# A hybrid conv, attention and mixture-of-experts step on one core: conditioning rows copied by ScalarE from two banks, tokens in three transfers, experts' weights placed in ten rounded columns

## What is computed

```
shift1, scale1, gate1, shift2, scale2, gate2 = split(silu(c) @ w_ada + b_ada)
h = rms_norm(x, norm1) * (1 + scale1) + shift1
conv_in, q_lat, kv_lat, k_rope, gates = split_projection(h @ w_in)
...                                  # conv branch, attention branch, merge
x = x + gate1 * ((g_conv * conv_out + g_att * att) @ w_out)
h2 = rms_norm(x, norm2) * (1 + scale2) + shift2
g_idx = argmax(h2 @ w_group); top two of the four experts of that group, weights comb
y = sum over the two experts of comb * (silu(h2 @ w1) * (h2 @ w3)) @ w2
x = x + gate2 * y
```

## Time and profile before

| | us |
|---|---|
| median of three runs | 976.42 |
| lowest, highest | 973.01, 978.05 |
| the profiled execution | 973.11 |
| its span in the trace | 971.3 |

### The profile page before, as it was taken

One profiled execution on the slowest core, in us unless ns is written; L12 is line 12 of the kernel. 1 busy time (PEld: TensorE's weight loads), 2 busy tenths in 40 slices (PEclk: granted clock), 3 DMA queues, 4 the chain that ended last, 5 costly groups with the idle time before them and its releaser, 6 DMA issues.

```text
span 971.3 us, 15302 instructions
## 1 busy us (share of the span) xinstructions
PE 920.6 (95%) x5910; PEld 776.3 (80%) x5910; DVE 737.4 (76%) x1208; ACT 512.0 (53%) x728; POOL 63.4 (7%) x62
## 2 busy tenths in 40 slices
PE   3999999989999899999989999998999989999997
PEld 1798889767898678888868988995589968788886
DVE  4665999564855799778967579995658568997895
ACT  4353822375522577647756346326663247774772
POOL 1000000064000000000010000001800000000000
PEclk9899999999999999999999999999999999999999
DMA  9943557401555689949927444531123247994961
GB/s 373 412 151 129 206 214 293 184 1 44 207 227 217 232 310 368 361 167 351 373 106 306 180 170 159 226 136 44 44 91 130 84 154 279 383 368 159 348 260 66
DMA packets 29018, 206.73 MB, mean 213 GB/s; under 512 B 3408, under 2 KB 3440, under 8 KB 4240
## 3 DMA queue, kind: packets, MB, share of 16 engines
q1 hardware_dynamic: 28656, 204.81, 55.2%
q0 software_dynamic: 288, 0.92, 0.3%
HBM read 203.98 MB, written 1.74 MB: 212 GB/s over the span
## 4 chain that ended last, share of the span: by engine, by line
PE 79%; DVE 10%; ACT 6%; issue 3%; DMA 1%; POOL 1%; ACTq 0%; SPq 0%; DVEq 0%
PE ps L875 59%; PE ps L886 4%; PE ps L862 3%; PE ps L1300 2%; PE ps L853 2%; DVE w_lo L743 2%; DVE w_lo L738 2%; ACT w_hi L732 2%; PE ps L1041 1%; PE ps L1129 1%; PE ps L1117 1%; POOL probs L832 1%; PE ps L1369 1%; PE ps L1370 1%; ACT kT L1563 1%
## 5 line engine op out<-in xcount | busy, mean ns | idle before, releaser
L743 DVE TENSOR_TENSOR w_lo<-ring,w_hi 128x2048 fp32r<-128x2048 f32 (+1 forms) x100 | 224.0, 2246 | 25.0 <-ACT w_hi L1670 24.5
L875 PE MATMUL ps<-h_hi,w_hi 128*128 128x384 f32 x576 | 198.0, 344 | 6.1 <-issue 2.4
L1670 ACT ACTIVATE w_hi<-ring 128x2048 fp32r<-128x2048 f32 x96 | 183.2, 1914 | 30.6 <-PE ps L875 30.6
L875 PE MATMUL ps<-h_hi,w_lo 128*128 128x384 f32 x576 | 193.6, 336 | 0.0
L875 PE MATMUL ps<-h_lo,w_hi 128*128 128x384 f32 x576 | 193.5, 336 | 0.0
L738 DVE TENSOR_TENSOR w_lo<-ring,w_hi 128x2048 fp32r<-128x2048 f32 x46 | 104.9, 2288 | 27.5 <-ACT w_hi L732 27.5
L875 PEld LDWEIGHTS ps<-h_hi,w_hi 128*128 128x128 f32 x576 | 108.0, 188 | 19.4 <-issue 11.7
L875 PEld LDWEIGHTS ps<-h_lo,w_hi 128*128 128x128 f32 x576 | 108.2, 188 | 0.0
L875 PEld LDWEIGHTS ps<-h_hi,w_lo 128*128 128x128 f32 x576 | 108.1, 188 | 0.0
L1916 DVE SCALAR_TENSOR_TENSOR z<-u,par,z 128x399 f32<-128x399 f32 x180 | 103.1, 629 | 0.9
L875 PE MATMUL ps<-w_hi,hg_hi 128*128 128x512 f32 x256 | 103.3, 404 | 0.0
(11 more groups left out here) (283 smaller groups left out, 1484.9 us busy)
## 6 DMA issues: line engine op xcount, KB each, us to landing
ring<-wpre SPq DMA_DIRECT2D x96, 1024.0 KB, 6.6
ring<-wmoe SPq DMA_DIRECT2D x96, 1024.0 KB, 5.8
x<-x SPq DMA_DIRECT2D x1, 1536.0 KB, 7.6
x_out<-x SPq DMA_DIRECT2D x4, 384.0 KB, 2.3
par<-par_in POOLq DMA_DIRECT2D x2, 367.5 KB, 6.8
const<-const_in SPq DMA_DIRECT2D x1, 314.0 KB, 3.2
ckv_out<-ckvT POOLq DMA_DIRECT2D x2, 64.0 KB, 3.7
kr_out<-kr POOLq DMA_DIRECT2D x2, 16.0 KB, 3.5
```

Source lines behind the costliest of these rows:

```text
L743: return nc.vector.tensor_tensor(out, whole, leading.bitcast(F32), ALU.subtract)
L875: m = mm(out, a, b, start=(start and i == 0 and j == 0), stop=(stop and i == n - 1 and j == 2))
L1670: af(w_hi[m % MOE_PLACES], slot(moe_slot(l, m)), ACT.Copy).then_inc(split_hi, 1)
```

## The change

- **Copies.** In layer 0 ScalarE takes over the copy of the conditioning rows from VectorE (`first_copy`), and the batches take turns in two banks (FIRST_BANKS), so that TensorE waits for the batch before the last only.
- **Order.** TensorE does the sum of squares first, then batches 0 and 1 whole, then the latent products of chunks 0 and 1; batches 2 and 3 follow with one chunk between rows and columns of each, and chunks 4 to 7 come last. ScalarE splits lat 1 behind chunk 1 (before: 3). VectorE makes the reciprocal in one instruction, without the copy between two parts.
- **Transfers.** Order is now cond, x in three parts (chunks 0 to 3, 4 and 5, 6 and 7), const. cond has its own semaphore, on which ScalarE's SiLU waits alone. GpSimd issues par only after the last part of x has landed.
- **Experts' weights.** VectorE splits `cwr` into two rounded halves (`cw_parts`, two more instructions and one more wait ahead of `cw_ready`); TensorE gathers the ten columns with fp32r operands; VectorE copies one half and adds the other (one more instruction).

```
-            sp.dma_start(cond_sb[:, :, :], cond).then_inc(loaded, 16)
+            sp.dma_start(cond_sb[:, :, :], cond).then_inc(cond_loaded, 16)
+            for (a, b), landed in zip(X_PARTS, x_loaded):
+                sp.dma_start(x[:, a:b, :], x0[:, a:b, :]).then_inc(landed, 16)
             sp.dma_start(const[:, :], const_in).then_inc(loaded, 16)
-
-            sp.dma_start(x[:, :, :], x0).then_inc(x_loaded, 16)
...
         def _(pool):
+            pool.wait_ge(x_loaded[-1], 16)
             pool.dma_start(par, par_in[0]).then_inc(par_loaded, 16)
...
-                    if k == 0:
-
-                        pe.wait_ge(adaT_taken, b)
-                    m = ada_rows_of(raw_unit("first", k * FIRST_STEPS + b), k, 2)
+                    if k == 0 and b >= len(FIRST_BANKS):
+
+                        pe.wait_ge(adaT_taken, b - len(FIRST_BANKS) + 1)
+                    m = ada_rows_of(raw_unit("first", k * FIRST_STEPS + b), k, 2, bank=FIRST_BANKS[b % 2])
...
                 if l == 0:
+                    square_sum()
                     first_rows(0, 0)
-                    square_sum()
                     first_rows(0, 1)
-                    ada_columns(1)
+                    ada_columns(1, bank=FIRST_BANKS[0])
+                    first_rows(1, 0)
+                    first_rows(1, 1)
+                    ada_columns(2, bank=FIRST_BANKS[1])
                     outs = [begin("lat", t) for t in range(TT)]
-                    for b in range(1, FIRST_STEPS):
+                    latent(0, outs)
+                    latent(1, outs)
+                    for b in range(2, FIRST_STEPS):
                         first_rows(b, 0)
                         first_rows(b, 1)
-                        ada_columns(b + 1)
-                        latent(2 * b - 2, outs)
-                        latent(2 * b - 1, outs)
-                    latent(KD - 2, outs)
-                    latent(KD - 1, outs)
+                        latent(b, outs)
+                        ada_columns(b + 1, bank=FIRST_BANKS[b % 2])
+                    for c in range(KD - 4, KD):
+                        latent(c, outs)
...
-                    n = EPG + 1
+                    n = 2 * (EPG + 1)
                     for b in range(PAIR):
-                        m = product(ps[:, 7, FE + b * n:FE + (b + 1) * n], [pick[:, t, b * P:(b + 1) * P].bitcast(F32) for t in range(TT)],
-                                    [cwr[:, t, :] for t in range(TT)])
+                        m = product(ps[:, 7, FE + b * n:FE + (b + 1) * n], [pick[:, t, b * P:(b + 1) * P] for t in range(TT)],
+                                    [cw_parts[:, t, :, :].rearrange("p s n -> p (s n)") for t in range(TT)])
...
+                def first_copy(b):
+                    act.wait_ge(ada_full, b + 1)
+                    if b:
+                        act.wait_ge(adaT_full, b)
+                    af(ada_rows, ps[:, FIRST_BANKS[b % 2], 0:ADA_COLS], ACT.Copy).then_inc(ada_taken, 1)
...
+                    if l == 0:
+                        first_copy(0)
+                        act.wait_ge(loaded, 16)
                     hi(1 if l > 0 else 0)
...
-                        if l == 0 and c == 3:
+                        if l == 0 and c == 1:
+                            first_copy(1)
                             hi(1)
+                        if l == 0 and c in (3, 5):
+                            first_copy(c // 2 + 1)
...
+                    mark(nc.vector.reciprocal(rs[:, 0:TOK], rs[:, 0:TOK]))
                     if l == 0:
-                        mark(nc.vector.reciprocal(rs[:, CTX:TOK], rs[:, CTX:TOK]))
-                        ada_copy(1)
-                        mark(nc.vector.reciprocal(rs[:, 0:CTX], rs[:, 0:CTX]))
-                        first_gain(0, False)
-                        dve.wait_ge(dve_order, count[0])
-                    else:
-                        chain(nc.vector.reciprocal(rs[:, 0:TOK], rs[:, 0:TOK]))
+                        first_gain(0)
+                    dve.wait_ge(dve_order, count[0])
...
-                    vt(cwr[:, :, 0:EPG], cw, cw2, ALU.add).then_inc(cw_ready, PAIRS)
+                    chain(vt(cwr[:, :, 0:EPG], cw, cw2, ALU.add))
+                    chain(copy(cw_parts[:, :, 0, :], cwr))
+                    lower(cw_parts[:, :, 1, :], cwr, cw_parts[:, :, 0, :]).then_inc(cw_ready, PAIRS)
...
-                    copy(cwg, ps[:, 7, FE:FE + PAIR * (EPG + 1)].rearrange("p (b n) -> p b n", b=PAIR)).then_inc(cwg_taken, 1)
+                    src = ps[:, 7, FE:FE + PAIR * 2 * (EPG + 1)].rearrange("p (b s n) -> p b s n", b=PAIR, s=2)
+                    chain(copy(cwg, src[:, :, 0, :]))
+                    vt(cwg, cwg, src[:, :, 1, :], ALU.add).then_inc(cwg_taken, 1)
```

More of the change, by code:

```diff
@@ L76 @@
 ADA_BANK = 7
+X_PARTS = ((0, 4), (4, 6), (6, 8))
+FIRST_BANKS = (ADA_BANK, 0)
 COND_AT = 32 - 2
@@ L552, in build @@
         cwr = v3(rt(TT * (EPG + 1)), TT)
+        cw_parts = place("cw_parts", TT * 2 * (EPG + 1), F32R, at=kr_at).rearrange("p (t s n) -> p t s n", t=TT, s=2)
         cwg = v3(rt(PAIR * (EPG + 1)), PAIR)
@@ L574, in slot @@
             return ring[:, s * UNIT:(s + n) * UNIT]
+        cond_loaded = sem("cond_loaded")
         loaded = sem("loaded")
-        x_loaded = sem("x_loaded")
+        x_loaded = [sem(f"x_loaded{n}") for n in range(len(X_PARTS))]
         u_cleared = sem("u_cleared")
@@ L818, in _ @@
                 pool.wait_ge(par_loaded, l * 16 + 16)
-                pool.wait_ge(loaded, 32)
+                pool.wait_ge(loaded, 16)
                 nc.gpsimd.tensor_tensor(conv_diag, fold.unsqueeze(1).broadcast_to([P, TAPS, QUAD]),
@@ L878, in split_product, with ada_rows_of @@
                 return m
-            def ada_rows_of(w, u, units, halves=(0, 1)):
+            def ada_rows_of(w, u, units, halves=(0, 1), bank=ADA_BANK):
                 w = v3(w, KD)
@@ L885, in ada_rows_of @@
                     for j in range(4):
-                        m = mm(ps[32 * j:32 * j + 32, ADA_BANK, 0:ADA_COLS], condp[:, 2 * j + c, at:at + 32], w[:, 2 * j + c, :],
+                        m = mm(ps[32 * j:32 * j + 32, bank, 0:ADA_COLS], condp[:, 2 * j + c, at:at + 32], w[:, 2 * j + c, :],
                                start=(u == 0 and c == 0), stop=(u == units - 1 and c == 1))
@@ L890, in ada_rows_of, with ada_columns @@
                 return m
-            def ada_columns(batches, at=0):
+            def ada_columns(batches, at=0, bank=ADA_BANK):
                 pe.wait_ge(ada_taken, batches)
                 for c in range(2):
-                    m = mm(ps[:, ADA_BANK, at + c * 32:at + (c + 1) * 32], ada_rows[:, c * P:(c + 1) * P], fold, start=True, stop=True)
+                    m = mm(ps[:, bank, at + c * 32:at + (c + 1) * 32], ada_rows[:, c * P:(c + 1) * P], fold, start=True, stop=True)
                     if c == 0:
@@ L899, in ada_columns @@
                 m.then_inc(adaT_full, 1)
-            pe.wait_ge(loaded, 32)
+            pe.wait_ge(loaded, 16)
             pe.wait_ge(condp_ready, 1)
@@ L1447, in rewind @@
                     count[0] = 0
-            act.wait_ge(loaded, 32)
+            act.wait_ge(cond_loaded, 16)
             af(cond_sb[:, :, :], cond_sb[:, :, :], ACT.Silu).then_inc(cond_ready, 1)
@@ L1456, in _ @@
                 base16 = landed16(act, done)
-                act.wait_ge(x_loaded, 16)
                 def hi(n):
                     make_hi(act, l, base, base16, n)
+                def first_copy(b):
[3 more added lines that the diff above has]
+                    af(ada_rows, ps[:, FIRST_BANKS[b % 2], 0:ADA_COLS], ACT.Copy).then_inc(ada_taken, 1)
                 def norm():
@@ L1467, in norm @@
                         act.wait_ge(x_moe, done * KD + (c + 1))
+                        for (a, _), landed in zip(X_PARTS, x_loaded):
+                            if l == 0 and c == a:
+                                act.wait_ge(landed, 16)
                         af(h[:, c, :], x[:, c, :], ACT.Square).then_inc(sq_ready, 1)
@@ L1761, in _ @@
             nc.vector.memset(rounds, 0).then_inc(set_up, 1)
-            dve.wait_ge(loaded, 32)
             dve.wait_ge(cond_ready, 1)
             copy(condp[:, :, COND_AT:COND_AT + 2], cond_sb[:, :, :]).then_inc(condp_ready, 1)
+            dve.wait_ge(loaded, 16)
             mark(vs(oh_r[:, TT, :], const[:, 0:GROUPS], 0.0, None, ALU.mult))
@@ L1783, in first_finish @@
                 dve.wait_ge(adaT_full, b + 1)
-                src = ps[:, ADA_BANK, 0:64].rearrange("p (c u s) -> p c u s", c=2, s=2)[:, :, 0:2, :]
+                src = ps[:, FIRST_BANKS[b % 2], 0:64].rearrange("p (c u s) -> p c u s", c=2, s=2)[:, :, 0:2, :]
                 out = mod[:, 0:2 * ADA_FIRST, :].rearrange("p (k b c) s -> p b c k s", k=2, c=2)[:, b]
@@ L1819, in gain, with first_gain @@
                                pf(name)[:, a:b].unsqueeze(2).broadcast_to([P, b - a, 2]), ALU.add, ALU.mult)
-                def first_gain(b, rows=True):
-                    if rows:
```

(2 more changed lines are left out.)

## The result

| | before | changed |
|---|---|---|
| median of 20 runs each, us | 977.38 | 972.50 |
| lowest, highest | 972.35, 986.25 | 966.04, 979.57 |
| the profiled execution | 973.11 | 971.09 |
| its span, granted clock | 971.3, 0.993 | 969.3, 0.991 |

The ratio is 0.9949, 95% interval 0.9926 to 0.9972: 5.0 us faster, 2.7 to 7.2 (the interval times 977.38), where 4.5 was forecast. The profiled executions differ by 2.0 us only, though, and the spread of either kernel's runs (14 us) is larger than the effect.

What follows compares the result with a forecast made beforehand. TensorE was taken as the bound (busy 95%, 79% of the chain). Front 2.7 plus gathers 1.8 gave 4.5 us, from the median 976.42 to 971.9; range 968.0 to 975.8.

Steps and rivals of the forecast that it cites:

- Transfers: Layer 0's front: parts of x land at 5.7, 6.6 and 7.6, const at 8.4; the reordering changes no byte in total.
- Squares at 5.7: Layer 0's front: ScalarE's squares start at 5.7 instead of 9.36, as x's first part lands earlier; 3.6 us won there.
- Batch 0's rows at 15.2: Layer 0's front: unit 1 lands at 14.2 and its conditioning rows on TensorE take 1.0 us.
- Batch 0 has slack: Layer 0's front: chunks 0 and 1 ready at about 22.6, not asked for before 25; up to 2.4 us delay costs nothing.
- The copy on ScalarE: Batch 1 in layer 0's front: ScalarE copies at 23.7, so latent products start 1.1 us earlier, 25.2 for 26.3.
- Clock: TensorE's clock in the front rises at 30.3 (bounds 28.6 and 32); 15 latent products run slow and 3 fast, ending at 30.9.
- Batches 2 and 3 and both limits: End of the front: batch 2's rows end at 32.8; TensorE's latent work and the last chain of splits meet within 0.4 us.
- The rival that goes over it: Clock rises early, unit 9's landing binds the front, first rounds gain more: 6.0 us, 970.4; chance 0.20.
- Gathers: Experts' weights: six fp32r instructions save 0.71 us per gather; 1.4 in second rounds, 0.4 in first, together 1.8 (0.6 to 2.8).
- ScalarE's list: Rival: front copies of batches 2 and 3 come late behind ScalarE's splits and h_hi; 2.5 us won, 973.9; chance 0.20.
- the rounded form saved what it should: Rival in the gathers: fp32r saves nothing and VectorE's added steps cost 0.4; 2.3 us won, 974.1; chance 0.05.
- the low clock did not stay through the front: Rival: clock stays at 1.2 GHz to the front's end, costing 11.7 against 4.5 won, 983.6; chance 0.05.

Runs made afterwards that it cites:

- early: Changed kernel with VectorE's wait for const moved behind the additions, so squares no longer stand behind const; ratio 0.9977 (0.9944 to 1.0009).
- vecopy: Changed kernel with the four copies of conditioning rows back on VectorE, two banks and new order kept; ratio 1.0006 (0.9976 to 1.0035).
- control: The changed kernel as it is, measured again in 12 runs; median 971.5 us, ratio 0.9944 (0.9905 to 0.9984).
- filled3: Changed kernel plus 13 extra products per layer, 3 of them right behind the second sum of squares; median 970.8 us, ratio 0.9962.
- filled: Changed kernel plus 15 extra fp32r products per layer whose results nobody reads; median 970.08 us, ratio 0.9926 (0.9896 to 0.9955).
- filled2: Changed kernel plus 10 extra products per layer, only where TensorE waits; median 971.25 us, ratio 0.9917 (0.9885 to 0.9949).
- best: Changed kernel plus 15 extra products per layer, early squares and three extra f32 products in layer 0's front; median 972.5 us, ratio 0.9968.

## Why the prediction was right, point by point

The total and its two terms came out (the front 2.8 to 3.3 us for 2.7, the gathers 1.9 for 1.8). On the way to the front's term three steps were wrong, and in the first trace they cancelled: that 25.37 met 25.2 is luck. That the end of the front holds against such errors is not, since two limits stand close behind it, as forecast.

- **Transfers: right.** Forecast 5.7, 6.6, 7.6 for the parts of x and 8.4 for const. Issue plus landing time in the page of the changed kernel:

```profile
x<-x SPq DMA_DIRECT2D x1, 768.0 KB, 4.5
x<-x SPq DMA_DIRECT2D x2, 384.0 KB, 5.3
const<-const_in SPq DMA_DIRECT2D x1, 314.0 KB, 5.9
```

  1.17 + 4.5 = 5.7 for the first part, 2.59 + 5.87 = 8.5 for const. The third part landed at 2.1 + 5.6 = 7.7. par took 7.0 from its issue at 8.0 (6.8 in its row before): the prediction's estimate of 2.9 for it fails, and par landed at 15.0, not at 10.5. A byte count at the stream's measured rate, from its effective start, was enough.
- **Squares at 5.7: wrong, and this is the first step that failed.** They started at 8.97. ScalarE's squares wait on x_moe, and VectorE gives that leave behind its own wait for const:

```profile
8.49 0.21 DVE L1792 TENSOR_SCALAR oh_r<-const 128x4 fp32r<-128x4 f32 x1 [5.66 <-DMA const<-const_in]
8.97 3.41 ACT L1489 ACTIVATE gates<-x 128x384 f32<-128x384 f32 x8 [6.36 <-DVEq L1816]
```

  (Timeline of the changed kernel.) The idle time of 6.36 us ended by VectorE's queue, not by a transfer, is the sign. I had listed the waits that the change edits and not the ones that stand unedited in the same loop. Moving const behind x thus undid what bringing x forward had won: 0.39 us were left of 3.6.
- **Batch 0's rows at 15.2: wrong too, and for another reason.** The forecast had one unit's rows there, 1.0 us. But TensorE's new list puts both units' rows behind the sum of squares, which before had the first of them ahead of it, and the trace of the kernel before gives 1.94 for each, not 1.0:

```profile
11.90 1.94 PE L886 MATMUL ps<-ring,condp 128*32 128x256 f32 x16 [11.90 <-DMA ring<-wpre]
16.07 1.94 PE L886 MATMUL ps<-ring,condp 128*32 128x256 f32 x16
```

  In the changed kernel they took 3.62, from 15.81 to 19.43, so the first scaled chunk came at 20.96: forecast 17.6, before 20.01. The new order thus made batch 0 0.95 us later than before. (1.8 to 1.9 for 16 is the pace that these rows have at low clock, 1.92 in the earlier trace rows, while the record shows full clock here; what slowed them is open.)
- **Batch 0 has slack: wrong as things came.** With the squares and the rows late, h_lo of chunks 0 and 1 ended at 25.2, not at 22.6, and VectorE's h_lo, not the columns of batch 1, released the latent products. The columns had been ready at 24.2, a microsecond before the forecast, since the clock was still full and batch 1's rows took 1.07, not 1.92. So errors both ways met at 25.37 against a forecast 25.2. The forecast sequence exists: `early` runs through it, with the low clock that it assumed, from 25.29 to 46.27 against 25.2 to 46.4, and is slower in the front for it.
- **The copy on ScalarE: right in kind, too small.** Forecast 1.1 us at batch 1 and no price for batch 3. `vecopy` shows 1.6 at batch 1 and 0.5 at batch 3.
- **Clock: right in size, not in kind.** Rise forecast at 30.3, seen at 30.2. But the forecast had the clock low ever since the waits and released by the dense work; it was full, fell at 26.8, with seven of the 18 dense products done, and rose 3.4 us later: 5.2 us for 5.7. That the dates agree is luck: the same front has its rise at 28.1, 28.3, 28.9 and 29.6 in `control`, `filled3`, `filled` and `filled2`. No row was behind the 30.3 nor its bound of 28.6. This and the next line are the 0.6 us by which 3.3 beats 2.7.
- **Batches 2 and 3 and both limits: right.** 30.56, 32.42 and 34.68 in the chain against 30.9, 32.8 and 35.2; the two limits meet (TensorE's latent work and the split of glu 0, which ended at 45.72). The third, unit 9, was forecast at 35.3 and landed at 35.4 to 35.7; it is on the chain where the clock rose early. The rival that goes over it had glu at 45.5; 45.70 is the earliest seen.
- **Gathers: right.** 0.67 and, in layer 1, 0.68 (lead 1.37 to 2.04) against 0.71. First rounds: from the sums of places to the next ones 77.95 and 78.28 in the two layers against 78.32 and 78.47, so 0.4 and 0.2 won against 0.2 each. Over all traces without low clock there, it is 77.88 to 78.07 with the new gather and 78.22 to 78.32 with the old one in layer 0, 78.10 to 78.45 and 78.32 to 78.51 in layer 1: the first is clear, the second within the scatter. VectorE went on at once behind the gather, as worked out: its split of the next unit starts 2.50 us behind the one before, 3.09 before the change.
- **The sum.** 2.7 + 1.8 = 4.5 forecast. 3.3 + 1.35 + 0.6 = 5.3 by positions (4.8 to 5.3 over the traces), 4.6 by the two lines at equal clock, 4.9 by the medians, each with some 0.3 or more of doubt. The range, 968.0 to 975.8, holds the median but not the runs; the text gave the short low stretch 1.4 us and the range, and did not know the long ones.
- The rivals: ScalarE's list did not bind (the copies of batches 2 and 3 came at 32.49 and 37.36, forecast 32.8 and 37.1), the rounded form saved what it should, and the low clock did not stay through the front.

## What to carry to other kernels

Before a transfer is brought forward, list every semaphore that its reader waits on, also the ones whose lines are not edited, and who gives them behind what: one unedited wait on VectorE took 3.3 of the 3.6 us off the squares' start here. And ask what stands next: with that wait moved (`early`, `best`) the front ended no more than 0.06 us earlier, since the landing of unit 9 limits it. A copy belongs on the engine whose list has nothing ahead of it when its input is ready; here that was worth some 2 us, most of it at batch 1. Before a loss in one trace is put down to an edit, take off what low clock did to the same rows. And where one kernel's runs spread by more than the effect, read the granted clock of each run beside its time: the position table of two traces shows where a lead is lost, and whether the loss has anything to do with the edit.

## What the runs showed of the hardware

- At the routing, behind a stretch of TensorE products one to twenty columns wide, the granted clock fell to the lower level in 11 of 14 traces at 316 to 323 us and in 13 at 783 to 791, for 3.4 us in most, 6.8 in three, but for 13.7 (twice), 27 and 31 us in some. The one of 27 us outlasts 19.5 us of gathers and dense products in which TensorE had no idle time (793.5 to 813.0, granted clock 0.50). It also fell in five traces at or soon behind the first scores of a layer (from 199 or 203, from 672 or 678 us), for 3.4 or 6.8 us. Each cost 1.5 us if short and 6.9 if 27 us long; this is most of the spread of 13 us between runs of one kernel.
- With fifteen wide products per layer that compute nothing, the clock was 0.993 and above in all of 10 runs of the changed kernel, but 0.987 to 0.996 in the 12 runs of `best`, which has them too, and 0.987 to 0.997 in the kernel before. With ten of them, where TensorE waits anyhow, none of 12 runs was over 973.5, without a cost at equal clock; with these ten and three more (`filled3`) 4 of 12 were. So that such products hold the clock is suggested by two sets of runs and contradicted by two others, and stays open.
- The changed kernel with the ten products (`filled2`) had the lowest ratio of all, 0.9917 (0.9885 to 0.9949), with no run over 972.9. Its median is within 1.3 us of the changed kernel's, and that it beats it is not shown.
